# Top-k search of a sparse-attention block: two of six key blocks counted on ScalarE by the sign of the difference

## The chip, the cores and the metric

One core of one Trainium2 chip. The time is the device time of one execution, in microseconds (us); of several runs the median is given. Engines are named as in the profile: PE is TensorE's matmuls, PEld its weight loads, DVE is VectorE, ACT is ScalarE, POOL is GpSimd, SP is SyncE (it issues the loads).

## What is computed

Two layers of a conformer-like block with sparse attention, and after them a third block of another kind (a gated recurrence and an MLP), which the change does not touch. What matters here stands in the first two layers, for 1024 tokens:

```
conv:      y = silu(layernorm(causal_conv(u_val * sigmoid(u_gate)))) @ w_pw2 * silu(g_conv)
indexer:   score[t, s] = sum over 8 heads of w[t, h] * relu(q_idx[t, h] . k_idx[s]),  s <= t
           sel = top_k(score[t], 256)
attention: softmax over the 256 selected keys only
out:       [y_conv, y_attn] @ w_out, norm, gate, residual
```

Queries are worked on in 8 blocks of 128. In blocks 0 and 1 no query has more than 256 keys, so all are kept. For blocks 2 to 7 the 256th largest score of each query must be found among 384, 512, 640, 768, 896 and 1024 keys, and ties beyond it are cut by position.

## The kernel before

Each engine has a queue of its own, written out by hand, and semaphores between them. PE's order in a layer is: projections of the latents, the scores, then the convolution side (`conv_in` of wg and wv, two halves each of two tiles; `conv_turn(0)`, that is transposes xt 0 to 3; conv 0, 1; wv of the second half; conv 2, 3; `gates(0)`; `conv_turn(1)`, xt 4 to 7; conv 4, 5; `gates(1)`; conv 6, 7; `gates_by_token(0)`; conv 8, 9, 10; `gates_by_token(1)`; `normed_turn`; the four gemms of pw2; `out_half` of the convolution's output), and then the attention, which needs the selection.

Matrices are multiplied in three bf16 products of high and low halves. The weights come in chunks of 128x2048 in a ring of three, and POOL splits each chunk n into w_hi (4 casts, L506) and w_lo (4 subtractions, L510) once PE has used chunk n-3.

PSUM tiles are shared: `big` has two tiles of 1024 columns, taken in turn, and `c` has four banks. A tile can be taken again when its last reader is done. So wv half 0 tile 0 waits for ACT's sigmoid of wg half 0 tile 0 (`glu_gate(0, 0)`), the second half's wg tiles wait for DVE's `glu(0, 0)` and `glu(0, 1)`, the g tiles of `gates(0)` wait for `glu(1, 0)` and `glu(1, 1)`, xt 4 to 7 wait for `conv_out(0)` to `conv_out(3)`, conv 4 and 5 wait for `conv_x(4)` and `conv_x(5)`, and conv 8 to 10 wait for `conv_out(4)` to `conv_out(6)`.

The selection runs on DVE. `f` holds, for each query (128 partitions) and each of the 6 blocks (columns), the bits of the threshold found so far. For each of 31 bits, from the top, four things happen, each closed by `step()` (DVE waits for its own last write): the candidate, f with the bit flipped (L1642); `count`, which compares every score with the candidate and sums the hits, one instruction for each block, six in all (L1525); whether 256 were reached (L1644); the bit taken into f (L1645). Then comes one more count and, block by block, the pass that marks the selected keys (L1655 to L1659: five instructions over the block's full width).

Between the bits DVE does the convolution's work: `beside(slot)` is called before bit 30-slot, and `beside(32 + j)` before the pass of block j. `conv_x(4)` to `conv_x(7)` stand in slot 18, `conv_stats` in slot 26, `split_normed` (the low halves of the normed activations, on which pw2 waits) in slot 30, and `gated_convolution(0..3)` (on the last of which `out_half` waits) in slots 32 to 35, in front of the passes of blocks 2 to 5. ACT has no part in the search: it waits for PE's tiles, in the order glu_gate, conv_x, gate, gate_by_token, `L1129` (layer norm), silu, copies.

Of the kernel before, what the change touches and what calls it, by code (L numbers as in the profile page):

```python
# [23 lines left out]
P = 128  # L24
# [69 lines left out]
def build(nc, ap, events):  # L94

    ctx = ExitStack()
    with ctx:
# [49 lines left out]
        s_sq = ctx.enter_context(nc.semaphore("sq"))  # L147
        s_rb_out = ctx.enter_context(nc.semaphore("rb_out"))
# [168 lines left out]
        TBS = range(2, NT)  # L317
        sc_at = [0, 0]
# [670 lines left out]
        def _(act):  # L989
# [28 lines left out]
            for l in range(LAYERS):  # L1018
# [91 lines left out]
                for half in range(2):  # L1110
                    glu_gate(half, 0)
                    glu_gate(half, 1)
                for q in range(4):
                    conv_x(q)
# [239 lines left out]
        def _(dve):  # L1354
# [99 lines left out]
            for l in range(LAYERS):  # L1454
# [67 lines left out]
                def count(thr, op=ALU.is_ge):  # L1522
                    for j, tb in enumerate(TBS):
                        N = (tb + 1) * P
                        ins = dve.tensor_scalar(is_over[tb], score[tb], thr(j), 0.0, op, ALU.add, accum_out=cnt[:, j:j + 1])  # L1525
                    step(ins)
# [64 lines left out]
                def beside(slot):  # L1591
# [4 lines left out]
                    if slot == 5:  # L1596
                        glu(0, 0)
                    if slot == 7:
                        glu(0, 1)
                    if slot == 10:  # L1600
                        if l == 0:
                            ada(1)
                        conv_pad()
                        for q in range(4):
                            conv_x(q)
                    if slot == 11:
                        conv_out(0)
                        conv_out(1)
                    if slot == 12:
                        glu(1, 0)  # L1610
                    if slot == 14:
                        glu(1, 1)
                        conv_out(2)
                    if slot == 15:
                        conv_out(3)
                    if slot == 18:
                        for q in range(4, 8):
                            conv_x(q)
                    if slot == 19:
                        conv_out(4)  # L1620
                        conv_out(5)
                    if slot == 22:
                        conv_out(6)
                        conv_out(7)
                    if slot == 26:
                        conv_out(8)
                        conv_out(9)
                        conv_out(10)
                        conv_stats()
                    if slot == 27:  # L1630
                        conv_shift()
                    if slot == 30:
                        split_normed(0)
                        split_normed(1)
                        split_normed(2)
                        split_normed(3)
                    if 32 <= slot < 36:
                        gated_convolution(slot - 32)

                for bit in range(30, -1, -1):  # L1640
                    beside(30 - bit)
                    step(dve.tensor_scalar(cand, f, 1 << bit, None, ALU.bitwise_xor))  # L1642
                    count(lambda j: cand[:, j:j + 1].bitcast(F32))
                    step(dve.tensor_scalar(hit, cnt, TOPK - 0.5, float(1 << bit), ALU.is_ge, ALU.mult))  # L1644
                    step(dve.tensor_tensor(f, f, hit, ALU.bitwise_xor))  # L1645

                beside(31)
                count(lambda j: f[:, j:j + 1].bitcast(F32), ALU.is_gt)
                step(dve.tensor_scalar(s_(S_KEEP, nb), cnt, -1.0, TOPK + 0.5, ALU.mult, ALU.add))
                for j, tb in enumerate(TBS):  # L1650
# [8 lines left out]
                    step(dve.tensor_scalar(score[tb], eq, -1.0, NEG, ALU.add, ALU.mult))  # L1659

# [359 lines left out]
```

## Time and profile before

| | |
|---|---|
| median of 3 runs | 3466.71 us (3465.79 to 3471.36) |
| the profiled execution's own time | 3461.7 us |
| its span, first to last instruction | 3459.9 us |
| mean granted TensorE clock | 0.940 |
| PE busy | 3064.8 us (89% of the span) |
| DVE busy | 1953.9 us (56%) |
| POOL busy | 961.7 us (28%) |
| ACT busy | 893.7 us (26%) |
| of DVE: the search's counts, L1525, x384 | 337.9 us |
| search and passes, layer 0 | 248.8 to 587.3 us |
| search and passes, layer 1 | 1054.2 to 1357.2 us |

An engine's busy time is summed over all stages. What a stage costs is read from the wait that ends last in it, and in the stages with the search PE, DVE and POOL each wait for one another.

### The profile page before, as it was taken

Reading aid. Unit: us, or ns where it says so; the run is one execution under the profiler, and the core shown is the slowest. Engines: PE = TensorE matmul, PEld = TensorE weight load, DVE = VectorE, ACT = ScalarE, POOL = GpSimd, SP = SyncE. Lnnn points to the kernel's source line nnn. Section 1 sums busy time; section 2 is a strip of 40 time slices with the busy share of each in tenths; the row PEclk is TensorE's granted clock in tenths of the full one; section 3 lists DMA queues with packets and bytes.
Section 4 is the critical chain, followed back from the end, with each engine's and each line's share of the span. In section 5 each row is a group of like instructions: output and inputs, shape, how many; then the busy total and the mean of one; then the engine's idle time right before and its main releaser. Section 6 shows DMA issues by size and latency. Waiting matters only on the chain.

```text
span 3459.9 us, 48765 instructions
## 1 busy us (share of the span) xinstructions
PE 3064.8 (89%) x20177; PEld 1945.1 (56%) x20394; DVE 1953.9 (56%) x2977; ACT 893.7 (26%) x1544; POOL 961.7 (28%) x1046
## 2 busy tenths in 40 slices
PE   7889886988678977888699999999998899999997
PEld 7449762775338663875365465555555744444443
DVE  2586897564689996664636445365363433333334
ACT  2250022653351031653322222231221211010001
POOL 2201661002222661002232322322322223333330
PEclk9997998999799988999789999989999899999998
DMA  7222230001200330001211111111102111111101
GB/s 250 104 85 83 98 129 30 29 8 65 93 33 28 107 122 25 29 11 77 82 37 37 49 37 37 49 37 37 49 25 86 50 37 49 49 49 61 49 25 55
DMA packets 49165, 207.16 MB, mean 60 GB/s; under 512 B 4488, under 2 KB 9776, under 8 KB 32304
## 3 DMA queue, kind: packets, MB, share of 16 engines
q1 hardware_dynamic: 42288, 195.63, 16.0%
q10 hardware_dynamic: 6656, 8.39, 0.8%
q8 instruction: 162, 2.65, 0.3%
q14 instruction: 59, 0.48, 0.0%
HBM read 187.22 MB, written 16.79 MB: 59 GB/s over the span
## 4 chain that ended last, share of the span: by engine, by line
PE 68%; DVE 24%; issue 4%; ACT 2%; DMA 1%; POOL 1%; SPq 0%; DVEq 0%; ACTq 0%; POOLq 0%
PE big L264 15%; PE big L265 15%; PE big L263 15%; DVE arena L1525 6%; PE banks L263 4%; PE banks L264 4%; PE banks L265 4%; PE banks L948 3%; PE banks L821 2%; DVE arena L1683 2%; DVE arena L1515 2%; DVE arena L1410 1%; DVE arena L1691 1%; PE big L540 1%; PE banks L540 1%
## 5 line engine op out<-in xcount | busy, mean ns | idle before, releaser
L506 POOL CAST w_hi<-stage 128x512 bf16<-128x512 f32 x520 | 314.5, 647 | 2419.1 <-PE big L265 1742.9
L510 POOL TENSOR_TENSOR w_lo<-stage,w_hi 128x512 bf16<-128x512 f32 x520 | 652.5, 1285 | 0.0
L264 PE MATMUL big<-ht_lo,w_hi 128*128 128x512 bf16 x1381 | 527.5, 382 | 30.1 <-DVE ht_lo L1416 23.5
L265 PE MATMUL big<-ht_hi,w_lo 128*128 128x512 bf16 x1380 | 526.6, 382 | 1.4
L263 PE MATMUL big<-ht_hi,w_hi 128*128 128x512 bf16 x1359 | 518.4, 381 | 1.5
L263 PE MATMUL big<-w_hi,ht_hi 128*128 128x256 bf16 (+1 forms) x1274 | 386.1, 303 | 47.8 <-DVE ht_lo L1583 30.5
L264 PE MATMUL big<-w_lo,ht_hi 128*128 128x256 bf16 (+1 forms) x1274 | 385.9, 303 | 3.8 <-DVE ht_lo L1675 3.6
L265 PE MATMUL big<-w_hi,ht_lo 128*128 128x256 bf16 (+1 forms) x1276 | 386.1, 303 | 0.7 <-issue 0.4
L1525 DVE TENSOR_SCALAR_CACHE_REDUCE arena<-arena,smalli 128x384 bf16<-128x384 f32 (+5 forms) x384 | 337.9, 942 | 2.3
L263 PEld LDWEIGHTS big<-ht_hi,w_hi 128*128 128x128 bf16 x1408 | 140.4, 100 | 189.9 <-DVE ht_lo L1416 23.9
L265 PEld LDWEIGHTS big<-ht_hi,w_lo 128*128 128x128 bf16 x1408 | 138.7, 98 | 168.7 <-issue 4.7
L264 PEld LDWEIGHTS big<-ht_lo,w_hi 128*128 128x128 bf16 x1408 | 138.6, 98 | 162.6 <-issue 6.8
L263 PEld LDWEIGHTS big<-w_hi,ht_hi 128*128 128x128 bf16 x1280 | 151.8, 119 | 95.2 <-DVE ht_lo L1583 31.5
L263 PE MATMUL banks<-w_hi,arena 128*128 128x128 bf16 (+2 forms) x697 | 180.5, 278 | 22.8 <-DVE arena L1545 16.8
L264 PE MATMUL banks<-w_lo,arena 128*128 128x128 bf16 (+2 forms) x700 | 181.7, 279 | 0.4
L265 PE MATMUL banks<-w_hi,arena 128*128 128x128 bf16 (+2 forms) x699 | 181.2, 279 | 0.2
L263 PE MATMUL big<-w_hi,arena 128*128 128x256 bf16 (+1 forms) x509 | 166.9, 328 | 16.3 <-DVE arena L1870 16.1
L1228 ACT ACTIVATE arena<-big 128x1024 f32<-128x1024 f32 x64 | 65.5, 1023 | 446.7 <-PE big L265 446.5
L265 PEld LDWEIGHTS big<-w_hi,ht_lo 128*128 128x128 bf16 x1280 | 151.3, 118 | 41.4 <-issue 4.7
L264 PEld LDWEIGHTS big<-w_lo,ht_hi 128*128 128x128 bf16 x1280 | 151.2, 118 | 40.8 <-issue 3.9
L265 PE MATMUL big<-w_hi,arena 128*128 128x256 bf16 (+1 forms) x507 | 166.1, 328 | 0.3
L264 PE MATMUL big<-w_lo,arena 128*128 128x256 bf16 (+1 forms) x506 | 165.7, 328 | 0.2
(294 smaller groups left out, 5862.2 us busy)
## 6 DMA issues: line engine op xcount, KB each, us to landing
stage<-in_w SPq DMA_DIRECT2D x130, 1024.0 KB, 4.8
arena<-in_w_ada SPq DMA_DIRECT2D x48, 512.0 KB, 4.2
arena<-in_x SPq DMA_DIRECT2D x16, 512.0 KB, 7.1
xs<-arena SPq DMA_DIRECT2D x16, 512.0 KB, 2.6
arena<-xs SPq DMA_DIRECT2D x16, 512.0 KB, 7.9
gt<-arena ACTq DMA_DIRECT2D x16, 256.0 KB, 2.6
arena<-gt ACTq DMA_DIRECT2D x16, 256.0 KB, 2.7
out_x<-arena SPq DMA_DIRECT2D x8, 512.0 KB, 2.7
```

The lines of the kernel that those rows point to most:

```text
L263: pe.matmul(out, ah, bh, start=start, stop=False)
L264: pe.matmul(out, ah, bl, start=False, stop=False)
L265: return pe.matmul(out, al, bh, start=False, stop=stop)
L506: pool.tensor_copy(w_hi[:, n % RING, c0:c1], stage[:, n % RING, c0:c1]).then_inc(s_w_hi_split, mark(s_w_hi_split, n, q))
L510: ins = pool.tensor_tensor(w_lo[:, n % RING, c0:c1], stage[:, n % RING, c0:c1], w_hi[:, n % RING, c0:c1], ALU.subtract)
L540: ins = pe.matmul(g[:, (n * 4 + q) * 8 + k:(n * 4 + q) * 8 + k + 1], ada_buf(i)[:, k % 2, q * P:(q + 1) * P], s_(S_C + k), start=True, sto ...
L821: ins = pe.transpose(g[:, (s - q0) * P:(s - q0 + 1) * P], PB[h % 2][:, s * P:(s + 1) * P], ident)
L948: ins = pe.matmul(g[:, s * 64:(s + 1) * 64].rearrange("p (j h) -> p j h", h=h), KF[c][:, s * P:(s + 1) * P], q, start=True, stop=True)
L1228: act.activation(out, tile(pool, *key)[:, :], func, **kw).then_inc(s_read_act, mark(s_read_act, *key))
L1515: dve.scalar_tensor_tensor(score[tb], PB[i % 2][:, 0:N], w, score[tb], ALU.mult, ALU.add).then_inc(s_acc, mark(s_acc, l, i))
L1525: ins = dve.tensor_scalar(is_over[tb], score[tb], thr(j), 0.0, op, ALU.add, accum_out=cnt[:, j:j + 1])
L1683: dve.tensor_tensor_reduce(PB[h % 2][:, 0:N], tile("big", "lg", l, tb, h)[:, 0:N], mask_of(tb), 1.0, -NEG, ALU.add, ALU.min, s_(S_NMX + h ...
```

## The change

For blocks 6 and 7 (columns 4 and 5, 896 and 1024 keys) the count of each of the 31 bits moves to ACT: `Sign(candidate - score)` over the block's width with a summed output, two instructions for a bit. The sum is at most N - 2*256 + 1.5 when 256 scores or more lie above the candidate. DVE writes ACT's two candidates first and signals `s_cand`, counts its four blocks, and at the start of the next bit waits for `s_sign` and takes ACT's two counts into f (`sign_counts`: two comparisons of one column each, one xor). ACT passes through the 31 bits in its own queue, with the convolution's glu_gate and conv_x calls at fixed slots; gate(0), gate(1) and conv_x(4..7) come behind the last bit. Since a sum of signs counts an equal score by a half, an end on DVE follows for the two blocks: a count of all six blocks, `next_up` (12 small instructions), a count of the two, `at_least_f` (2), a count of the two again.

DVE's convolution work is placed anew: glu(0, 0) from slot 5 to 9, glu(0, 1) from 7 to 12, conv_x(0..3) from 10 to 18, conv_out(0) and (1) from 11 to 19 and 20, glu(1, 0) from 12 to 22, glu(1, 1) from 14 to 25, conv_out(2) and (3) from 14 and 15 to 27 and 28, conv_x(4..7) from 18 to 31, conv_out(4) and (5) from 19 to 33. conv_out(6) and all behind it (statistics, split_normed, gated_convolution) come after the last pass.

```
@@ ACT's queue: behind the relus of the scores @@
-                for half in range(2):
-                    glu_gate(half, 0)
-                    glu_gate(half, 1)
-                for q in range(4):
-                    conv_x(q)
+                def beside(slot):
+                    if slot == 4:
+                        glu_gate(0, 0)
+                    if slot == 7:
+                        glu_gate(0, 1)
+                    if slot == 15:
+                        glu_gate(1, 0)
+                    if slot == 17:
+                        glu_gate(1, 1)
+                    if slot == 18:
+                        for q in range(4):
+                            conv_x(q)
+
+                for bit in range(30, -1, -1):
+                    beside(30 - bit)
+                    act.wait_ge(s_cand, when(s_cand, l, bit))
+                    for j in ON_ACT:
+                        tb = TBS[j]
+                        ins = act.activation(is_over[tb], score[tb], ACT.Sign, scale=-1.0, bias=smalli[:, 8 + j:9 + j].bitcast(F32), accum_out=s_(S_CNT + j))
+                    ins.then_inc(s_sign, mark(s_sign, l, bit))
                 gate(0)
                 gate(1)
@@ DVE's queue @@
+                def next_up():
+                    up, lo, hi = [smalli[:, 24 + 8 * i:24 + 8 * i + a1 - a0] for i in range(3)]
+                    fa = f[:, a0:a1]
+                    step(dve.tensor_scalar(hit[:, a0:a1], cnt[:, a0:a1], TOPK - 0.5, None, ALU.is_ge))
...
+                    step(dve.tensor_tensor(fa, hi, lo, ALU.bitwise_or))
+
+                def at_least_f():
+                    keep = smalli[:, 24:24 + a1 - a0]
+                    step(dve.tensor_scalar(keep, cnt[:, a0:a1], TOPK - 0.5, -1.0, ALU.is_ge, ALU.mult))
+                    step(dve.tensor_tensor(f[:, a0:a1], f[:, a0:a1], keep, ALU.bitwise_and))
+
+                def sign_counts(bit):
+                    dve.wait_ge(s_sign, when(s_sign, l, bit))
+                    for j in ON_ACT:
+                        most = (TBS[j] + 1) * P - 2 * TOPK + 1.5
+                        ins = dve.tensor_scalar(hit[:, j:j + 1], cnt[:, j:j + 1], most, float(1 << bit), ALU.is_le, ALU.mult)
+                    step(ins)
+                    step(dve.tensor_tensor(f[:, a0:a1], f[:, a0:a1], hit[:, a0:a1], ALU.bitwise_xor))
 
                 for bit in range(30, -1, -1):
+                    if bit < 30:
+                        sign_counts(bit + 1)
+                    dve.tensor_scalar(cand[:, a0:a1], f[:, a0:a1], 1 << bit, None, ALU.bitwise_xor).then_inc(s_cand, mark(s_cand, l, bit))
                     beside(30 - bit)
-                    step(dve.tensor_scalar(cand, f, 1 << bit, None, ALU.bitwise_xor))
-                    count(lambda j: cand[:, j:j + 1].bitcast(F32))
-                    step(dve.tensor_scalar(hit, cnt, TOPK - 0.5, float(1 << bit), ALU.is_ge, ALU.mult))
-                    step(dve.tensor_tensor(f, f, hit, ALU.bitwise_xor))
+                    step(dve.tensor_scalar(cand[:, 0:a0], f[:, 0:a0], 1 << bit, None, ALU.bitwise_xor))
+                    count(lambda j: cand[:, j:j + 1].bitcast(F32), which=on_dve)
+                    step(dve.tensor_scalar(hit[:, 0:a0], cnt[:, 0:a0], TOPK - 0.5, float(1 << bit), ALU.is_ge, ALU.mult))
+                    step(dve.tensor_tensor(f[:, 0:a0], f[:, 0:a0], hit[:, 0:a0], ALU.bitwise_xor))
+                sign_counts(0)
 
                 beside(31)
-                count(lambda j: f[:, j:j + 1].bitcast(F32), ALU.is_gt)
+                thr_f = lambda j: f[:, j:j + 1].bitcast(F32)
+                count(thr_f, ALU.is_gt)
+                next_up()
+                count(thr_f, ALU.is_ge, ON_ACT)
+                at_least_f()
+                count(thr_f, ALU.is_gt, ON_ACT)
@@ behind the passes of the six blocks @@
+                conv_out(6)
+                conv_out(7)
+                conv_out(8)
+                conv_out(9)
+                conv_out(10)
+                conv_stats()
+                conv_shift()
+                for n in range(4):
+                    split_normed(n)
+                for n in range(4):
+                    gated_convolution(n)
```

## Rows read from the trace of the kernel before

**Rows 1.** Stages, by window: us; PE, PEld, DVE, ACT, POOL busy (instructions); PEclk; DMA share; GB/s

```profile
248.80:415.30 166.50, 158.36 (x1244) 142.44 (x1244) 126.07 (x289) 11.35 (x15) 60.58 (x72) 0.86 0.27 91
415.30:481.50 66.20, 61.38 (x586) 47.49 (x588) 59.95 (x131) 4.43 (x6) 42.22 (x52) 0.95 0.35 114
481.50:570.00 88.50, 50.98 (x318) 33.19 (x320) 82.42 (x135) 27.36 (x31) 34.17 (x37) 0.82 0.23 82
570.00:617.00 47.00, 46.43 (x236) 22.08 (x240) 16.79 (x15) 8.28 (x9) 9.46 (x13) 0.95 0.06 23
1054.20:1184.80 130.60, 115.73 (x1000) 102.72 (x1000) 125.97 (x284) 11.36 (x15) 59.68 (x72) 0.95 0.19 65
...
1252.80:1339.90 87.10, 51.22 (x319) 33.11 (x322) 81.22 (x135) 27.34 (x31) 33.38 (x36) 0.81 0.24 80
```

**Rows 2.** Waits, layer 0: engine, line <- releaser: us in total, times, longest

```profile
DVE arena L1666 <- ACT arena L1165: 30.8, 1, 30.8
...
PE big L263 <- DVE ht_lo L1583: 15.3, 1, 15.3
PE banks L263 <- DVE arena L1545: 6.8, 2, 6.0
PE big L263 <- POOL w_lo L510: 6.7, 2, 4.8
```

**Rows 3.** Timeline of DVE, one bit with POOL idle: start us, us

```profile
248.76 0.17 DVE L1642 TENSOR_SCALAR smalli<-smalli 128x6 int32<-128x6 int32 x1
248.97 0.61 DVE L1525 TENSOR_SCALAR_CACHE_REDUCE arena<-arena,smalli 128x384 bf16<-128x384 f32 x1
...
251.91 1.14 DVE L1525 TENSOR_SCALAR_CACHE_REDUCE arena<-arena,smalli 128x896 bf16<-128x896 f32 x1
...
254.29 0.17 DVE L1644 TENSOR_SCALAR smalli<-small 128x6 int32<-128x6 f32 x1
...
254.70 0.17 DVE L1642 TENSOR_SCALAR smalli<-smalli 128x6 int32<-128x6 int32 x1
```

**Rows 4.** Timelines of POOL and DVE, a bit under a weight split

```profile
430.16 4.50 POOL L510 TENSOR_TENSOR w_lo<-stage,w_hi 128x512 bf16<-128x512 f32 x4
...
431.15 0.20 DVE L1644 TENSOR_SCALAR smalli<-small 128x6 int32<-128x6 f32 x1
431.39 1.07 DVE L1645 TENSOR_TENSOR smalli<-smalli 128x6 int32<-128x6 int32 x1
432.49 1.08 DVE L1642 TENSOR_SCALAR smalli<-smalli 128x6 int32<-128x6 int32 x1
```

**Rows 5.** Timeline of DVE, layer 1: slot 18

```profile
1184.80 2.48 DVE L1545 TENSOR_TENSOR arena<-banks,arena 128x512 bf16<-128x512 f32 x4
```

**Rows 6.** Groups of ACT by shape: xcount | busy us, mean ns | idle before

```profile
L1206 ACT ACTIVATE arena<-arena,small 128x1024 f32<-128x1024 f32 x16 | 18.4, 1150 | 28.2 <-DVE small L1683 28.2
...
L1206 ACT ACTIVATE arena<-arena,small 128x896 f32<-128x896 f32 x16 | 16.7, 1043 | 23.3 <-DVE small L1683 23.3
```

**Rows 7.** Timelines of DVE and ACT, layer 0: PE's tiles arrive; a table load

```profile
296.55 1.23 DVE L1533 TENSOR_TENSOR arena<-big,arena 128x1024 f32<-128x1024 f32 x1 [13.80 <-PE big L265]
...
320.65 1.23 DVE L1533 TENSOR_TENSOR arena<-big,arena 128x1024 f32<-128x1024 f32 x1 [11.13 <-PE big L265]
...
351.91 1.02 ACT L1062 ACTIVATE arena<-big 128x1024 f32<-128x1024 f32 x1 [9.45 <-PE big L265]
...
354.91 1.28 ACT L1075 ACT_TABLE_LOAD   x1
```

**Rows 8.** Timeline of DVE, the selection pass of width 896

```profile
575.01 0.69 DVE L1655 TENSOR_SCALAR arena<-arena,smalli 128x896 f32<-128x896 f32 x1
...
580.17 0.63 DVE L1659 TENSOR_SCALAR arena<-arena 128x896 f32<-128x896 f32 x1
```

**Rows 9.** Timeline of POOL, a split beside the selection

```profile
557.32 6.89 POOL L510 TENSOR_TENSOR w_lo<-stage,w_hi 128x512 bf16<-128x512 f32 x4
```

**Rows 10.** Timeline of DVE, behind the batch statistics

```profile
487.38 12.22 DVE L1642 TENSOR_SCALAR smalli<-smalli 128x6 int32<-128x6 int32 x1
```

More of the change, by code:

```diff
@@ L317, in build @@
         TBS = range(2, NT)
+        ON_ACT = (NT - 4, NT - 3)
         sc_at = [0, 0]
@@ L1521, in _, with count @@
                 cnt = s_(S_CNT, nb)
-                def count(thr, op=ALU.is_ge):
-                    for j, tb in enumerate(TBS):
-                        N = (tb + 1) * P
+                on_dve = [j for j in range(nb) if j not in ON_ACT]
+                a0, a1 = ON_ACT[0], ON_ACT[-1] + 1
+                def count(thr, op=ALU.is_ge, which=range(nb)):
+                    for j in which:
+                        tb = TBS[j]
                         ins = dve.tensor_scalar(is_over[tb], score[tb], thr(j), 0.0, op, ALU.add, accum_out=cnt[:, j:j + 1])
@@ L1595, in beside @@
                         gate_gain(1)
-                    if slot == 5:
+                    if slot == 9:
                         glu(0, 0)
-                    if slot == 7:
+                    if slot == 12:
                         glu(0, 1)
-                    if slot == 10:
+                    if slot == 17:
                         if l == 0:
@@ L1612, in beside @@
                         glu(1, 1)
+                    if slot == 27:
                         conv_out(2)
-                    if slot == 15:
+                    if slot == 28:
                         conv_out(3)
-                    if slot == 18:
+                    if slot == 31:
                         for q in range(4, 8):
                             conv_x(q)
-                    if slot == 19:
+                    if slot == 33:
                         conv_out(4)
                         conv_out(5)
-                    if slot == 22:
-                        conv_out(6)
-                        conv_out(7)
@@ L1625, in beside @@
[L1625 to L1638, printed above, removed]
+                def next_up():
+                    up, lo, hi = [smalli[:, 24 + 8 * i:24 + 8 * i + a1 - a0] for i in range(3)]
+                    fa = f[:, a0:a1]
+                    step(dve.tensor_scalar(hit[:, a0:a1], cnt[:, a0:a1], TOPK - 0.5, None, ALU.is_ge))
+                    step(dve.tensor_scalar(up, fa, 31, None, ALU.arith_shift_right))
+                    step(dve.tensor_scalar(up, up, 2.0, 1.0, ALU.mult, ALU.add))
+                    step(dve.tensor_tensor(up, up, hit[:, a0:a1], ALU.mult))
+                    step(dve.tensor_scalar(lo, fa, 0xFFFF, None, ALU.bitwise_and))
+                    step(dve.tensor_tensor(lo, lo, up, ALU.add))
+                    step(dve.tensor_scalar(hi, fa, 16, None, ALU.arith_shift_right))
+                    step(dve.tensor_scalar(up, lo, 16, None, ALU.arith_shift_right))
+                    step(dve.tensor_tensor(hi, hi, up, ALU.add))
+                    step(dve.tensor_scalar(hi, hi, 16, None, ALU.logical_shift_left))
+                    step(dve.tensor_scalar(lo, lo, 0xFFFF, None, ALU.bitwise_and))
+                    step(dve.tensor_tensor(fa, hi, lo, ALU.bitwise_or))
```

10 lines of the change are left out of this document (7 added, 3 removed).

## The prediction

> **What bounds the kernel now.** I read the stage windows first, then PE's waits, then the timelines of DVE, POOL and ACT. The windows [rows 1] cut each layer at the same four places: the search's first bit, slot 18 (`conv_x(4)`), the end of conv 10, and the start of `out_half`. In layer 0 the stages take A 166.5, B 66.2, C 88.5 and D 47.0 us; in layer 1 A 130.6, B 68.0 (what lies between its neighbours) and C 87.1. DVE is busy 76% and 96% of A, 90% of B, 93% of C. Even so the selection is not what the attention waits for: in layer 0 the last pass ends at 587.3, and DVE's first instruction of the attention then idles 30.8 us [rows 2]. What counts is when DVE serves the convolution. PE waits 6.0 us for `conv_x(4)` (L1545, at the end of A), 15.3 us for the last `gated_convolution` (L1583, at the end of C) and up to 4.8 us for POOL's splits (L510) [rows 2]. So a faster search is worth nothing as such; the change is worth what its new order does to these three waits.
>
> **One bit.** With POOL idle a bit takes 254.70 - 248.76 = 5.94 us: the four narrow counts 251.91 - 248.97 = 2.94, the two wide ones 254.29 - 251.91 - 0.11 = 2.27, the last count's end 0.11, the three small steps 0.21, 0.21 and 0.20 [rows 3]. The change takes out 2.27 and adds four small instructions: two comparisons and the candidate for ACT, 0.1 each where nothing is waited for between them, and two closed steps of 0.2 that take one of these in; in sum 0.6. New bit: 5.94 - 2.27 + 0.6 = 4.27 us. ACT needs 1.04 + 1.15 for two activations of these widths with summed outputs and a pointer for bias, and 0.19 for the last read-out: 2.4 us [rows 6]. DVE works 3.7 us between sending ACT's candidates and wanting the sums, so ACT is hidden by 1.3 us, if Sign from SBUF costs what Exp from SBUF does. Without that cover each us beyond 3.7 would cost 62 us.
>
> **A bit under a split.** While POOL splits a chunk, each small instruction ends at the next end of a POOL instruction. POOL's subtractions come every 4.50 / 4 = 1.12 us, and the steps take 1.07 and 1.08 in place of 0.2; only the first, which falls in anywhere, took 0.20 [rows 4]. The counts are not held up. Casts come about every 0.56, so a POOL instruction is 0.84 on the mean. Now three small ones follow one another. Over A of layer 1, 130.6 us hold 18 bits (106.9), the work beside them (9.2) and a wait of some 2: 12.4 us are left for POOL's 59.7 us of work [rows 1]. That is 0.21 per us of POOL, or 1.55 per bit under a split, 0.52 for each small instruction. After the change seven follow one another: 7 x 0.52 = 3.6. A bit under a split costs 4.27 + 3.6 = 7.9, against 5.94 + 1.55 = 7.5 now. The bit that shrinks by 28% beside an idle POOL grows beside a busy one, and 46% of POOL's time (3.6 / 7.9) becomes delay. Only the one-column comparisons could escape, since no row has that shape; then five count, 2.6 a bit, 38%. I take seven, as the nearest row (six columns) waits.
>
> The Trainium skill, page "SBUF — State Buffer", section "Who interferes with whom", says that tensor_scalar, but not its accumulating form, and tensor_tensor with two SBUF inputs contend with GpSimd, and that the loser blocks for the whole instruction. The trace agrees with which ones wait (L1642 and L1645 1.08 and 1.07, L1525 0.61 as ever). By whole instructions, 7 x 0.84 less half of one for the first, less the 1.2 they take anyway, the delay is 4.2 a bit, and the forecast below would be some 4 us higher.
>
> **Stage A, layer 1.** `conv_x(4)` moves from slot 18 to slot 31. 31 x 4.27 = 132.4; beside it four glu (1.23 [rows 7] less an overlap of 0.1), conv_x 2.5 [rows 5], four conv_out at about 0.5: 9.1; POOL's work on the nine chunks up to g1, 60 us, at 46%: 27.6. Slot 31 comes at 1054.2 + 169.1 = 1223.3, against 1184.8 [rows 5]: +38.5. DVE waits for nothing in it; PE waits for glu(0, 0), glu(0, 1) and conv_x(0), which all come later than now. ACT then has a table load (1.28 [rows 7]), two Silu of the width of the sigmoid (1.02 [rows 7]) and a copy at 0.55 to do behind its last sum, of which 2 us stick out: **+40**.
>
> **Stage A, layer 0.** Here PE is slow to deliver. Slots 0 to 8: 9 x 4.27 + 2.3 (gate_gain) + 6.7 x 0.46 = 43.8, to 292.6; glu(0, 0) waits until 296.5 and glu(0, 1) until 320.6, for the same tiles as now [rows 7]. Slots 12 to 14 end near 337.6. In 15 and 17 ACT stands before wg tiles of the second half; the last comes at 351.9, then sigmoid 1.0 and the sums 2.4: slot 18 at 355.4. Thirteen bits 55.5, beside them 6.7, POOL's seven chunks less a part, 43.5 us, at 46%: 20. Slot 31 at 437.6, +2 as above, against 415.3: **+24**.
>
> **Stage B.** Between conv 4 and conv 10 PE is 93% busy [rows 1] and already waits for POOL. Now DVE's counts let POOL run. Afterwards this stage meets the end of the search: 12 + 2 small steps and, from about 20 us behind slot 31, the six passes, whose instructions are of the kind that contends, at full width. The pass of width 896 takes 5.8 us for five [rows 8]; by width all six take 27 us, 0.9 for each of the 30. Where such a pass meets a split now, POOL's four subtractions take 6.89 in place of 4.50 [rows 9], though the passes there are interrupted by instructions on PSUM. Uninterrupted, they alternate: a chunk of 8 instructions takes 6.7 + 8 x 0.9 = 14. The split of g2, for which PE waits, and those of cv8 and cv9, behind which cv10's queues, fall in here: **+7 and +7, +14 in each layer**, both for PE directly. The bound from below is 0, from the counts beside which POOL is not slowed; the passes are those of rows 9, so I take the whole.
>
> **Stage C.** Statistics, split_normed and gated_convolution no longer stand behind bits and passes. The low halves follow ACT's copies at once, the layer norm no longer waits for slot 27, and pw2 starts 5 us earlier; the 15.3 us before out_half shrink to the chain of one product (1.23), one copy (1.08) and one subtraction (1.15): 3.5. **-16** in layer 0, **-15** in layer 1. PE starts D behind a shorter idle time; 192 matmuls at 0.216 are 41.4 of the 47.0 us there, and I give back **-2** in each layer.
>
> **Sum.** Layer 0: 24 + 14 - 16 - 2 = +20. Layer 1: 40 + 14 - 15 - 2 = +37. The moves of glu and conv_out are in A; the semaphores cost nothing more (a satisfied wait shows no gap). No DMA is moved; the loads only follow POOL. +57 on the profiled execution's 3461.7 us gives 3519, and it ran 5.0 below the median of the runs, so 3524. With five small instructions A gives 3 and 5 less, 3516; own range 3508 to 3540.
>
> **Rivals.**
> - POOL is not held up by the passes: B costs 0, the sum is +29, 3496. For it: POOL's casts are hardly longer there. Against: rows 9. Chance 0.17.
> - The small steps don't queue (narrower shapes, or POOL's splits fall beside the counts): the other side. A gives +5 and +14, B 0, C and D as above: -16, 3451. It decides where a small step costs under 0.1 us for POOL, not 0.52, and the passes let POOL through. Against it: every burst in rows 4 waits. Chance 0.09.
> - Starvation: behind the batch statistics a small instruction waited 12.22 us until POOL ran out of work, past eight of its boundaries [rows 10]. ACT's candidate is followed directly by DVE's own. Should that pair starve the same way, a bit is held through each of POOL's runs: about another 60 us, 3580. Every other step behind an unclosed one waited for one boundary only. Chance 0.06.
> - ACT decides: a sum is late and DVE waits for it. If Sign and Sigmoid don't share a table, four slots a layer pay two loads of 1.28 and 1 for the sigmoid, of which 1.3 is covered: +2.3 x 8 = 18, 3542. The Trainium skill, page "ScalarE: Activation LUTs", section "Table sets: the hidden batching unit", says tables are switched by named sets at about 2.7 us; it doesn't list Sign. Chance 0.07.
>
> **How the numbers follow.** The forecast has 0.58, with 3524 its value; the remaining 0.03 is for no change by gains and losses that cancel. About 0.2% (7 us) is what a measurement here can tell. Slower is the sum of forecast, POOL let through, starvation and ACT: 0.88; faster 0.09; same 0.03. The range must leave out the other side and starvation; it reaches down to POOL let through and up to ACT: 3488 to 3546.
>
> **What the profile would show.** A new bit of 4.2 to 4.4 us beside an idle POOL, and 7 to 9 beside a busy one; two activations of 1.04 and 1.15; conv_x(4) at about 438 and 1224; PE's wait before conv 4 grown from 6 to some 20 us; a split of 12 us or more during the passes; PE's idle time before out_half down to 3.5. The prediction is wrong if bits under a split stay below 6 us, if ACT's sums are waited for, or if POOL's chunks keep 6.7 us.

## The result, and the profile after

The median goes from 3467.8 us (3465.8 to 3471.4, four runs) to 3490.5 us (3489.7 to 3495.8, four runs): a ratio of 1.0068, interval 1.0050 to 1.0085. The change costs 22.7 us. I had forecast 3524, so the direction was right and the size was not. The profiled execution of after took 3489.7 us (span 3487.9), 28.0 us of span more than before; the terms below are read from these two executions, and some 5 of the 28 are that before's ran 6 us under its median, after's only 1.

First the stages, cut where [rows 1] cut them: search's first bit, start of `conv_x(4)`, end of conv 10, start of `out_half`. Columns as there.

```profile
249.70:435.10 185.40, 161.63 (x1244) 145.39 (x1244) 154.71 (x485) 81.05 (x138) 60.67 (x72) 0.82 0.26 87
435.10:510.10 75.00, 63.19 (x586) 48.34 (x588) 64.97 (x75) 5.79 (x9) 59.66 (x53) 0.93 0.27 92
510.10:579.80 69.70, 50.25 (x318) 33.17 (x320) 24.43 (x31) 27.30 (x31) 28.56 (x34) 0.84 0.24 84
...
1059.40:1221.50 162.10, 116.82 (x1000) 102.19 (x1000) 153.55 (x479) 81.14 (x138) 60.81 (x72) 0.87 0.17 59
1221.50:1297.20 75.70, 64.17 (x586) 48.84 (x588) 66.28 (x76) 5.83 (x9) 60.97 (x53) 0.91 0.27 93
1297.20:1365.30 68.10, 48.59 (x318) 32.47 (x320) 25.18 (x31) 27.30 (x31) 28.13 (x34) 0.90 0.24 83
```

| stage | forecast, layers 0 and 1 | measured | 
|---|---|---|
| A, to conv_x(4) | +24, +40 | +18.9, +31.5 |
| B, to the end of conv 10 | +14, +14 | +8.8, +7.7 |
| C, to out_half | -16, -15 | -18.8, -19.0 |
| D, to the attention's first product | -2, -2 | -0.9, -0.2 |
| sum | +57 | +28 |

The sum of the measured terms equals the difference of the spans; what lies outside the four stages (+0.9 us ahead of layer 0, -3.7 between the layers, +2.8 behind) cancels. In B POOL is busy 59.7 us for the 42.2 of [rows 1], with the same chunks: the splits take longer there, which is already visible in one column.

Waits of layer 0 (engine, line, releaser: us in total, times, longest), to set beside [rows 2]:

```profile
PE banks L265 <- DVE arena L1565: 19.6, 2, 14.7
PE big L265 <- POOL w_lo L513: 9.8, 2, 5.7
...
PE banks L265 <- POOL w_lo L513: 5.1, 2, 4.0
PE big L265 <- DVE ht_lo L1603: 4.7, 1, 4.7
```

L1565 is `conv_x`: TensorE's wait before conv 4 grew from 6.0 to 14.7 us (in layer 1 from 4.9 to 15.2), and the one before conv 0 from 0.8 to 4.9 (in layer 1 from 5.1 to 14.4). L1603 is the last gated convolution: 15.3 became 4.7.

One bit beside an idle POOL (timeline of VectorE, start and duration), which took 5.94 in [rows 3]:

```profile
1059.37 0.17 DVE L1678 TENSOR_SCALAR smalli<-smalli 128x2 int32<-128x2 int32 x1
...
1062.91 0.16 DVE L1683 TENSOR_TENSOR smalli<-smalli 128x4 int32<-128x4 int32 x1
1063.10 0.21 DVE L1671 TENSOR_SCALAR smalli<-small 128x1 int32<-128x1 f32 x2
1063.35 0.16 DVE L1673 TENSOR_TENSOR smalli<-smalli 128x2 int32<-128x2 int32 x1
1063.55 0.17 DVE L1678 TENSOR_SCALAR smalli<-smalli 128x2 int32<-128x2 int32 x1
```

1063.55 - 1059.37 = 4.18 us. Now the same steps under a split, VectorE and then POOL, to set beside [rows 4]:

```profile
1181.53 0.53 DVE L1678 TENSOR_SCALAR smalli<-smalli 128x2 int32<-128x2 int32 x1
1181.97 0.65 DVE L1680 TENSOR_SCALAR smalli<-smalli 128x4 int32<-128x4 int32 x1
...
1185.70 0.27 DVE L1682 TENSOR_SCALAR smalli<-small 128x4 int32<-128x4 f32 x1
1186.01 1.07 DVE L1683 TENSOR_TENSOR smalli<-smalli 128x4 int32<-128x4 int32 x1
1187.11 0.21 DVE L1671 TENSOR_SCALAR smalli<-small 128x1 int32<-128x1 f32 x2
1187.36 0.83 DVE L1673 TENSOR_TENSOR smalli<-smalli 128x2 int32<-128x2 int32 x1
1188.22 0.53 DVE L1678 TENSOR_SCALAR smalli<-smalli 128x2 int32<-128x2 int32 x1
```

```profile
1181.42 2.29 POOL L509 CAST w_hi<-stage 128x512 bf16<-128x512 f32 x4
1183.67 4.50 POOL L513 TENSOR_TENSOR w_lo<-stage,w_hi 128x512 bf16<-128x512 f32 x4
```

This bit takes 1188.22 - 1181.53 = 6.69 us, not 7.9. Five steps are stretched, but the pair of one-column comparisons (L1671) is not: 0.21 to 0.22 us for both, in each of the 62 times that the two layers run it. No small step of a bit takes over 1.45 us in this trace. ScalarE's counts, beside it:

```profile
1182.09 1.04 ACT L1131 ACTIVATE arena<-arena,smalli 128x896 bf16<-128x896 f32 x1 [3.87 <-DVE smalli L1678]
...
1183.13 1.13 ACT L1131 ACTIVATE arena<-arena,smalli 128x1024 bf16<-128x1024 f32 x1
```

With the last read-out they end 1.3 us before VectorE's last count. Last, the splits beside the passes in layer 0, POOL and then VectorE:

```profile
463.88 3.54 POOL L509 CAST w_hi<-stage 128x512 bf16<-128x512 f32 x4 [9.80 <-PE big L267]
467.38 7.07 POOL L513 TENSOR_TENSOR w_lo<-stage,w_hi 128x512 bf16<-128x512 f32 x4
474.40 5.05 POOL L509 CAST w_hi<-stage 128x512 bf16<-128x512 f32 x4
479.42 7.61 POOL L513 TENSOR_TENSOR w_lo<-stage,w_hi 128x512 bf16<-128x512 f32 x4
486.98 4.86 POOL L509 CAST w_hi<-stage 128x512 bf16<-128x512 f32 x4
491.80 8.87 POOL L513 TENSOR_TENSOR w_lo<-stage,w_hi 128x512 bf16<-128x512 f32 x4
```

```profile
466.98 0.78 DVE L1699 TENSOR_SCALAR arena<-arena,smalli 128x640 f32<-128x640 f32 x1
467.80 2.33 DVE L1700 TENSOR_TENSOR_SCAN arena<-arena 128x640 f32<-128x640 f32 x1
470.16 1.59 DVE L1701 SCALAR_TENSOR_TENSOR arena<-arena,small 128x640 f32<-128x640 f32 x1
```

Three chunks take 10.6, 12.6 and 13.7 us instead of 6.7. The first is g2's, for which TensorE waits 5.7; the second is split while TensorE works on g2's four tiles (22.6 us) and costs nothing; of the third 1.1 sticks out, and for conv 10's chunk, queued behind it, TensorE waits 4.0. In before it waits 1.9 for g2's chunk and 1.9 for conv 10's. The net is 3.8 and, with the 1.1, 3.2 us; the remaining 1.8 of B's 8.8 is TensorE's own busy time, 63.2 for 61.4 us.

### The profile page after: what moved, and what is told of

It reads as the page before. It is cut to its first block, busy times and chain, and to the rows that moved or that the text cites. A ratio compares the mean times of both kernels' runs of the same rounds, so it can differ in the third digit from the quotient of the medians.

```text
span 3487.9 us, 49110 instructions
## 1 busy us (share of the span) xinstructions
PE 3070.3 (88%) x20177; PEld 1950.1 (56%) x20394; DVE 1873.4 (54%) x3021; ACT 1032.9 (30%) x1792; POOL 995.9 (29%) x1046
## 4 chain that ended last, share of the span: by engine, by line
PE 68%; DVE 21%; issue 5%; POOL 3%; ACT 2%; DMA 1%; SPq 0%; DVEq 0%; ACTq 0%; POOLq 0%
PE big L266 16%; PE big L267 15%; PE big L265 15%; DVE arena L1545 4%; PE banks L265 4%; PE banks L266 4%; PE banks L267 4%; PE banks L951 3%; PE banks L824 2%; POOL w_lo L513 2%; DVE arena L1738 2%; DVE arena L1533 2%; DVE arena L1428 1%; POOL w_hi L509 1%; DVE arena L1746 1%
## 5 line engine op out<-in xcount | busy, mean ns | idle before, releaser
L509 POOL CAST w_hi<-stage 128x512 bf16<-128x512 f32 x520 | 330.6, 679 | 2414.0 <-PE big L267 1702.2
L513 POOL TENSOR_TENSOR w_lo<-stage,w_hi 128x512 bf16<-128x512 f32 x520 | 671.0, 1322 | 0.0
L265 PE MATMUL banks<-w_hi,arena 128*128 128x128 bf16 (+2 forms) x697 | 182.0, 280 | 60.8 <-DVE arena L1565 49.3
L1545 DVE TENSOR_SCALAR_CACHE_REDUCE arena<-arena,smalli 128x512 bf16<-128x512 f32 (+5 forms) x268 | 206.7, 827 | 2.3
L1131 ACT ACTIVATE arena<-arena,smalli 128x896 bf16<-128x896 f32 x124 | 134.9, 1089 | 185.8 <-DVE smalli L1678 185.7
```

What stands on the lines that cost most here:

```text
L265: pe.matmul(out, ah, bh, start=start, stop=False)
L509: pool.tensor_copy(w_hi[:, n % RING, c0:c1], stage[:, n % RING, c0:c1]).then_inc(s_w_hi_split, mark(s_w_hi_split, n, q))
L513: ins = pool.tensor_tensor(w_lo[:, n % RING, c0:c1], stage[:, n % RING, c0:c1], w_hi[:, n % RING, c0:c1], ALU.subtract)
L1131: ins = act.activation(is_over[tb], score[tb], ACT.Sign, scale=-1.0, bias=smalli[:, 8 + j:9 + j].bitcast(F32), accum_out=s_(S_CNT + j))
```

## The experiments

Ratios are to the kernel before, from runs on the same chip; the kernel after stands at 1.0068. The runs were spread over several chips, so two of them are compared by their ratios (0.001 is 3.5 us) rather than by their medians.

| run | median us | ratio, interval |
|---|---|---|
| e1 passes last | 3477.0 | 1.0015 (1.0000 to 1.0029) |
| e2 before, passes last | 3442.2 | 0.9918 (0.9896 to 0.9939) |
| e3 two columns | 3497.2 | 1.0074 (1.0054 to 1.0094) |
| e4 one column | 3510.4 | 1.0112 (1.0090 to 1.0134) |
| e5 planned | 3424.8 | 0.9874 (0.9858 to 0.9889) |
| e6 planned, candidates by column | 3425.1 | 0.9871 (0.9850 to 0.9893) |
| e7 no exact end | 3483.6 | 1.0037 (1.0013 to 1.0060) |
| e8 planned, VectorE alone | 3433.9 | 0.9918 (0.9896 to 0.9939) |
| e9 before, statistics closed | 3465.4 | 0.9999 (0.9984 to 1.0015) |
| e10 e8 refitted | 3432.2 | 0.9911 (0.9896 to 0.9926) |
| e11 e5 refitted in layer 1 | 3425.3 | 0.9889 (0.9873 to 0.9906) |
| e12 e10 refitted | 3430.5 | 0.9890 (0.9874 to 0.9907) |

### Stages B and C: where the passes stand (e1, e2)

e1, on the kernel after:

```
                 count(thr_f, ALU.is_gt, ON_ACT)
                 step(dve.tensor_scalar(s_(S_KEEP, nb), cnt, ...))
-                for j, tb in enumerate(TBS):    # the six passes
-                    ...
+                conv_out(4)
+                conv_out(5)
                 conv_out(6)
                 ...
                 for n in range(4):
                     gated_convolution(n)
+                for j, tb in enumerate(TBS):
+                    ...
```

> Edit on the kernel after: the six selection passes move behind the four gated convolutions; the low convolution outputs 4 and 5 come behind the exact end. Theory (the passes hold up POOL's splits between conv 4 and conv 10): that stretch, 74.1 us in layer 0 and 74.8 in layer 1 in the kernel after against 65.3 and 67.1 in the kernel before, falls back to about 66 and 67; the passes (27 us) fit beside out_half, where VectorE idles 47 us; the total falls by about 16 us, to some 3474. Rival (the stretch is longer for another reason, the exact end's small steps or TensorE's clock): the stretch stays at 74 and the total within 5 us of the kernel after.

Measured 3477.0, by the ratios 18 us below after, where some 16 were expected. Stages A and B of layer 0, by window, and the four subtractions of a split in B, from POOL's timeline:

```profile
248.20:429.00 180.80, 157.27 (x1246) 141.00 (x1244) 156.01 (x485) 81.14 (x138) 60.68 (x72) 0.84 0.27 90
429.00:496.80 67.80, 63.17 (x588) 48.33 (x588) 26.04 (x45) 5.76 (x9) 42.75 (x53) 0.93 0.29 99
```

```profile
466.82 4.50 POOL L513 TENSOR_TENSOR w_lo<-stage,w_hi 128x512 bf16<-128x512 f32 x4
```

B falls from 75.0 to 67.8 (68.2 in layer 1), POOL's time in it from 59.7 to 42.8, a chunk is back at 6.7, while C (70.3 and 68.4) keeps its gain. In layer 0 1.6 us over before's 66.2 are left, and before's own B took 67.7 us in the trace of e2, whose B is unchanged: B's cost was the passes, as far as this can tell. A is the same code as after and took 180.8 here against 185.4: in this execution TensorE's second wv tile held VectorE for 7.1 us, in after's for 10.3. Layer 0's term A is therefore known to some 5 us only; layer 1's is 162.0 and 162.1.

e2, on the kernel before:

```
-                    if 32 <= slot < 36:
-                        gated_convolution(slot - 32)
...
+                for n in range(4):
+                    gated_convolution(n)
                 for j, tb in enumerate(TBS):    # the six passes
```

> Edit on the kernel before: the passes of all six blocks move behind the four gated convolutions, nothing else. Theory (what the change gains in stage C is that nothing stands between gated convolutions, and ScalarE's counting has no part in it): TensorE's wait before out_half falls from 15.3 to about 4.7 us in each layer, and the total by some 21 us, to about 3446. Rival (the wait is set by the search's 31 bits, which still end at 535, so that the chain through the layer norm is late): less than 5 us per layer.

Measured 3442.2, 27 us below before on the same chip, where 21 were expected. From TensorE's waits in layer 0:

```profile
PE big L263 <- DVE ht_lo L1583: 4.7, 1, 4.7
```

The 15.3 us are 4.7 without any count on ScalarE. From the end of conv 10 to out_half e2 takes 76.9 us in layer 0, 11.6 less than before, and 11.6 less in layer 1; the change gained 18.8 and 19.0. So 11.6 us of the gain in C came from the order of VectorE's queue, and before could have had them alone. The other 7, most of them from pw2 starting earlier, e2 does not give.

### Stage A: which small steps POOL holds up (e3, e4)

e3 and e4, on the kernel after:

```
# e3
-    ins = dve.tensor_scalar(hit[:, j:j + 1], cnt[:, j:j + 1], most, float(1 << bit), ALU.is_le, ALU.mult)
+    ins = dve.tensor_scalar(smalli[:, 48 + 2 * i:50 + 2 * i], cnt[:, a0:a1], most, float(1 << bit), ALU.is_le, ALU.mult)
# e4, and so for every small step of a bit
-    step(dve.tensor_tensor(f[:, 0:a0], f[:, 0:a0], hit[:, 0:a0], ALU.bitwise_xor))
+    for j in on_dve:
+        ins = dve.tensor_tensor(f[:, j:j + 1], f[:, j:j + 1], hit[:, j:j + 1], ALU.bitwise_xor)
+    step(ins)
```

> Edit on the kernel after: each of the two comparisons of ScalarE's sums runs over two columns instead of one, into a scratch tile. Theory (an instruction of one column escapes the queue with POOL, one of two columns does not): beside an idle POOL nothing changes (4.18 us a bit); beside a busy one the pair, now 0.21 us for both, takes 1 to 2 us; a bit under a split goes from 6.5 to about 7.6, the start of conv_x(4) moves by 4 us in layer 0 and 6 in layer 1, and the total rises by about 10 us. Rival (the pair escapes by its place or its data types, float in and integer out): the pair stays at 0.21 us and the total unchanged.

> Edit on the kernel after: every small step of a bit (candidates, comparisons, xors) is written as one instruction per column. Theory (one column escapes): a bit costs 4.18 plus about 1.1 for 11 more instructions, 5.3 us, beside an idle and a busy POOL alike, against 4.18 and 6.5 now; POOL's splits are not stretched; conv_x(4) comes some 10 us later in layer 1 and the total rises by 10 to 20 us. Rival (the comparisons escaped by place or type): single columns of the xors wait too, several boundaries of 1.1 us in each bit, 10 us and more for a bit under a split, and the total rises by over 40 us.

e3 took 3497.2. e4 took 3510.4, 20 us above after by the medians and 15 by the ratios, within its 10 to 20, with 4.8 us a bit beside an idle POOL where I had said 5.3. The pair in e3, under a split and then beside an idle POOL:

```profile
1191.05 1.08 DVE L1671 TENSOR_SCALAR smalli<-small 128x2 int32<-128x2 f32 x2
...
1198.98 0.24 DVE L1671 TENSOR_SCALAR smalli<-small 128x2 int32<-128x2 f32 x2
```

A bit's steps in e4, under a split:

```profile
1197.21 0.34 DVE L1689 TENSOR_SCALAR smalli<-small 128x1 int32<-128x1 f32 x4
1197.58 3.77 DVE L1692 TENSOR_TENSOR smalli<-smalli 128x1 int32<-128x1 int32 x4
...
1202.62 0.33 DVE L1685 TENSOR_SCALAR smalli<-smalli 128x1 int32<-128x1 int32 x4
```

Width decides for `tensor_scalar`: in one column it never waits (no group of four over 0.34 us), in two columns the same comparison takes up to 2.2 us for the pair. Layer 1's stage A is 1226.1 - 1060.0 = 166.1 us in e3 against 162.1: 4 of the 8.5 us by which I overstated it. (The total of e3, 1.0074, cannot be told from after's 1.0068; the stage can.) But one column does not free a `tensor_tensor`: four xors took 3.77 us, each but the first waiting for one more end of a subtraction of POOL (every 1.12 us). Both rival lines of e4 were half right. The Trainium skill has this in two places, "VectorE: DVE Perf Modes", section "What auto-detection actually checks" (the mode that uses both ports asks that source and destination have outermost non-unit dimensions that are even, or equal; one column, as I read it, has none) and "SBUF — State Buffer", section "Who interferes with whom" (`tensor_scalar` contends in those modes only, `tensor_tensor` with both inputs in SBUF without them). The traces agree with both; the prediction weighed the second page and left out its condition on `tensor_scalar`.

e6 uses it, on e5 below:

```
-    dve.tensor_scalar(cand[:, a0:a1], f[:, a0:a1], 1 << bit, None, ALU.bitwise_xor).then_inc(s_cand, ...)
+    for j in ON_ACT:
+        ins = dve.tensor_scalar(cand[:, j:j + 1], f[:, j:j + 1], 1 << bit, None, ALU.bitwise_xor)
+    ins.then_inc(s_cand, ...)
```

> Edit on e5_planned: the candidates (a tensor_scalar of two columns and one of four) are written as six of one column. Theory (a tensor_scalar of one column is not held by POOL, as the comparisons of 0.21 us for two show): beside an idle POOL a bit costs 0.2 us more, beside a busy one some 1.2 less; over 31 bits, nine of them under splits, 4 us less in a layer where the bits set the end, so 0 to 8 us less in all. Rival (the comparisons escape for another reason than their width): 0.2 x 31 = 6 us more per layer, up to 12 in all.

The candidates indeed never waited (0.21 to 0.22 us for two, up to 0.33 for four, in all 62 bits), and a bit beside an idle POOL became 4.4 us. The total cannot be told from that of e5. What the form is worth stays open: the five executions lie between 3411.8 and 3432.2 us, and in the profiled one, the slowest, two comparisons behind the counts took 8.76 and 7.58 us (see the section on the order, and the last).

### The exact end (e7)

The lines from `next_up()` to the last `count(thr_f, ALU.is_gt, ON_ACT)` are left out.

> Edit on the kernel after: the exact end (the 12 small steps, the two further counts of two blocks, the two steps of at_least_f) is left out, so that a threshold of blocks 6 and 7 can be off by one step where scores are equal; the first count of all six blocks stays. Theory (its 15 us lie on VectorE behind conv_x(4..7), where TensorE waits for nothing from it; it only shifts the passes against POOL's splits): the total within 5 us of the kernel after, and the passes hold up the split of g2 by more, those of cv8 and cv9 by less. Rival (it is on the path): 10 to 15 us less in each layer, 3465.

Measured 3483.6, 6.9 below after by the medians and 11 by the ratios, more than the 5 expected, though the two intervals still overlap. The passes start earlier and meet g2's split with their wide blocks: TensorE waits 8.2 us for it instead of 5.7, and 1.9 for conv 10's chunk instead of 4.0, as expected. From `conv_x(4)` to out_half the two layers take 144.6 and 143.5 us, in after 144.8 and 143.8. So in these stages the exact end costs 0.3 us at most; if the total did fall by more, this trace does not show where.

### The order fitted to TensorE, with and without ScalarE's counts (e5, e8, e10, e11, e12)

e5, on e1. The two tables name, for each layer, what is done beside which slot:

```
+PLAN_DVE = ({15: glu 0 0, 17: glu 0 1, 22: pad, x 0-3, 23: out 0, 26: out 1, glu 1 0, glu 1 1, out 2,
+             28: out 3, 30: x 4-7, out 4, out 5},
+            {7: glu 0 0, glu 0 1, pad, 12: x 0-3, 14: out 0, out 1, 17: glu 1 0, glu 1 1, out 2,
+             22: out 3, 24: x 4-7, 30: out 4, out 5})
+PLAN_ACT = ({3: gate 0 0, 11: gate 0 1, 21: gate 1 0, 22: gate 1 1, x 0-3, 30: g 0, g 1, x 4-7},
+            {0: gate 0 0, 3: gate 0 1, 10: gate 1 0, 12: gate 1 1, x 0-3, 22: g 0, g 1, 23: x 4-7})
+# behind the bits: out 6-10, conv_stats, conv_shift, the exact end, split_normed, gated_convolution, passes
```

> Edit on the kernel after: ScalarE still counts two blocks and the passes come last, as in the run e1_passes_last; the convolution's work is placed anew, in each layer by itself, so that glu, conv_x and conv_out come when TensorE's tiles are ready: conv_x(4..7) behind 30 bits in layer 0 and behind 24 in layer 1, glu(0, 1) in slot 17 and 7; ScalarE's gates and conv_x calls move with them; the exact end goes behind the layer norm's shift, where VectorE idles 20 us for ScalarE. Theory (what the change lost, it lost by the slots at which VectorE serves TensorE): TensorE's wait before conv 4, 14.7 and 15.2 us, falls to under 6 in layer 0 and under 10 in layer 1, conv 4 starts near 412 in layer 0, out_half starts some 35 and 25 us earlier than in the kernel after; total 3415, within 10. Rival (ScalarE's waits for TensorE's tiles inside the bits hold its sums, and VectorE with them): bits of over 8 us around those slots and a total over 3440.

Measured 3424.8, at the edge of the expected 10 around 3415: 46 us below before on the same chip, some 66 below after; this version beats both kernels. Stages A to C of layer 0, and TensorE's waits in layer 1:

```profile
249.50:412.40 162.90, 160.21 (x1247) 143.06 (x1244) 146.31 (x471) 78.98 (x134) 55.31 (x67) 0.85 0.28 93
412.40:476.00 63.60, 59.08 (x590) 44.96 (x588) 11.59 (x25) 7.98 (x13) 47.42 (x58) 1.00 0.36 120
476.00:545.70 69.70, 49.33 (x320) 32.61 (x320) 38.45 (x67) 27.32 (x31) 29.31 (x35) 0.90 0.25 88
```

```profile
PE banks L265 <- DVE arena L1562: 12.8, 2, 9.1
...
PE big L265 <- ACT arena L1080: 5.2, 1, 5.2
```

In layer 0 TensorE waits under 1 us for `conv_x(4)`, and in B the granted clock is 1.00, which is 2.4 GHz throughout, where it was 0.93 behind the wait of 14.7 us. Out_half starts 296 us behind the first bit instead of 330. In layer 1 9.1 us are left before conv 4.

e8 does the same with before's six counts on VectorE, e10 and e12 refit it where TensorE was seen to wait; e11 refits e5 in layer 1.

> Edit on the kernel before: VectorE counts all six blocks as ever and ScalarE has no part in the search; only VectorE's convolution work is placed anew, in each layer by itself (conv_x(0..3) from slot 10 to 14 and 9, conv_x(4..7) from 18 to 19 and 16, outputs 8 to 10 and the statistics at 27 and 24, the low halves at 30 and 29), and the passes come behind the gated convolutions. Theory (the order alone brings the gain of e5_planned, and the counts on ScalarE bring nothing): 3420, within 10, no slower than e5_planned (3425). Rival (31 bits of 5.94 us leave no order that serves both the middle and the layer norm in time): no better than e2_before_passes_last (3442).

> Edit on e8_planned_dve, in which TensorE waited 16.2 us for output 6 in layer 0 and 17.1 and 6.5 us for the low halves in layer 1: outputs 4, 5 come at slot 22 and 6, 7 at 25 in layer 0, output 5 at 19 and the low halves at 27 in layer 1, glu(0, 0) at 11 in layer 0. VectorE still counts all six blocks. Theory (the order is worth the whole gain): those waits shrink to about 5, 9 and 0, total 3412, within 10, below e5_planned. Rival (six counts on VectorE leave it too full: each slot moved makes another one late): 3430 or more.

> Edit on e10_planned_dve2 (VectorE counts all six blocks), where TensorE waited 17.2 us in layer 1 for a gated convolution that stood behind the last bits: there gated_convolution(0) and (1) come at slots 29 and 30, and the last count of all blocks comes behind the gated convolutions in both layers. Theory (the counts on ScalarE are worth nothing once the order is fitted): the 17.2 us fall to 2 or less, out_half of layer 1 starts some 15 us earlier, total 3417 within 8, ratio about 0.987 as for e5_planned and e11_planned2. Rival (VectorE with six counts stays the bound there, and gives the wait back elsewhere): 3428 or more, a ratio of 0.990 or more.

> Edit on e5_planned (two blocks counted on ScalarE), layer 1 alone: conv_x(0..3) at slot 11 instead of 12, outputs 0 and 1 at 13, glu(1, 0), glu(1, 1) and output 2 at 16, output 3 at 21, conv_x(4..7) at 22 instead of 24, and ScalarE's gate(2) and gate(3) in front of its slots 27 and 29 instead of behind all bits. Theory: TensorE's waits of 3.8 (conv 0), 9.1 (conv 4) and 5.2 us (gates_by_token) fall to about 1, 4 and 0; total 3412, within 8. Rival (ScalarE's waits inside the bits hold its sums and VectorE): 3425 or more. Against e10_planned_dve2 it tells what the counts on ScalarE are worth when both orders are fitted: this theory says nothing, within 10 us.

Their edits are entries of those tables only, but for e12, in which two gated convolutions go among the last bits and the last count goes behind them:

```
-                for n in range(4):
+                for n in ((0, 1, 2, 3), (2, 3))[l]:
                     gated_convolution(n)
+                count(lambda j: f[:, j:j + 1].bitcast(F32), ALU.is_gt)
+                step(dve.tensor_scalar(s_(S_KEEP, nb), cnt, -1.0, TOPK + 0.5, ALU.mult, ALU.add))
```

e8, e10 and e12 took 3433.9, 3432.2 and 3430.5: the theory's 3412 to 3420 was missed each time, and e11's 3412 too, with 3425.3. Layer 1 of e12, TensorE's waits:

```profile
PE banks L263 <- DVE arena L1555: 9.6, 1, 9.6
...
PE big L263 <- DVE ht_lo L1584: 9.3, 1, 9.3
...
PE big L263 <- DVE arena L1581: 4.1, 1, 4.1
```

The 17.2 us of e10 (L1581, gated convolution) became 4.1, and 9.6 for output 6 and 4.6 more before out_half came in their place. e11 went the same way: 9.1, 3.8 and 5.2 us became 4.3, 0.8 and 4.1, and new waits of 5.2 (a glu) and 3.9 (an output) appeared. With ScalarE's counts the two fitted orders stand at 0.9874 and 0.9889, without them the best two at 0.9890 and 0.9911. The best intervals overlap, so these runs put the worth of ScalarE's counts between nothing and some 13 us, against over 30 for the order.

The waits that I fitted the orders to were in large part not waits for the order. A step can starve, as in [rows 10]: it is not served until POOL has run out of work. The comparison behind the counts did so in e8, e12 and e6, one line from each (timeline of VectorE):

```profile
476.41 7.45 DVE L1622 TENSOR_SCALAR smalli<-small 128x6 int32<-128x6 f32 x1
```

```profile
1196.63 9.13 DVE L1624 TENSOR_SCALAR smalli<-small 128x6 int32<-128x6 f32 x1
```

```profile
424.02 8.76 DVE L1667 TENSOR_SCALAR smalli<-small 128x4 int32<-128x4 f32 x1
```

In e8 this step stands right before output 6, for which TensorE waited 16.2 us, and another of 8.04 us before it; a step of 11.4 us behind the statistics of layer 1 stands before the low halves (17.1). In e10 such a step of 12.2 us stands before the wait of 17.2. In layer 1 of e12 VectorE is busy without a gap from the 9.13 us to output 6, for which TensorE waited 9.6. In e5 no small step of a bit takes over 1.22 us, but in e11, also with ScalarE's counts, two take 5.9. With one trace of each, these runs cannot separate what a fuller queue costs from what such steps cost, so the 13 us are no measure of the counts alone.

### The starved step of rows 10 (e9)

```
                 ins.then_inc(s_stats, mark(s_stats, "var", l))
+                dve.wait_ge(s_stats, when(s_stats, "var", l))
```

> Edit on the kernel before: VectorE waits for its own last bn_aggr before it goes on, nothing else. Theory (the small step of rows 10 starves for 12.2 us because it is issued behind an instruction that is not closed, while POOL works): that step takes 1.1 us or less; slots 27 to 31 and the gated convolutions come 10 us earlier, TensorE's wait before out_half falls from 15.3 to about 5 in each layer, total 3447. Rival (it starves by its place beside the splits, whatever closes the work before it): 12 us again, in the wait or behind it, and the total unchanged.

```profile
495.63 0.64 DVE L1564 BATCH_NORM_AGGREGATE diag<-diag 128x2 f32<-128x6 f32 x8
496.30 12.11 DVE L1643 TENSOR_SCALAR smalli<-smalli 128x6 int32<-128x6 int32 x1
```

Measured 3465.4 and a step of 12.11 us (11.28 in layer 1): my theory fell. See the last section.

## Why the prediction was right in sign and twice too large

**The bit.** Forecast 4.27 beside an idle POOL, measured 4.18; over 31 bits that is 2.8 us a layer.

**The failed step: "I take seven, as the nearest row (six columns) waits", and with it 7.9 us for a bit under a split.** In stage A of layer 1, 162.1 us are 31 x 4.18 = 129.6, the work beside the bits 9.1 and 2.2 of waiting for ScalarE's copy; 21.2 are left for POOL's 60.8: 0.35 us of delay for each us of POOL, not 0.46, and a bit under a steady split is 4.18 / 0.65 = 6.4. The forecast had 27.6 for these 21.2. The direct test is e3: widening the pair to two columns gives 4 of the missing 8.5 us back. The price of five, which stood in the prediction as its lower case (21 and 35), was the nearer one. In layer 0 the term was 24 for 18.9.

**Stage B** had the right mechanism (e1 removes it, to within 1.6 us) at 14 us a layer instead of 8.8 and 7.7. I charged g2's split and conv 10's with a full alternation (14 us a chunk). g2's met the narrow passes, at 10.6; of the delay of the two chunks before conv 10's most was hidden by TensorE's 22.6 us on g2's tiles, which I had not set against it. Net of before's waits the two cost 3.8 and 3.2 us in layer 0, where I had 7 and 7.

**Stage C** went as forecast and 3 to 4 us further: pw2 starts 5.9 us nearer to the end of the gates by token, out_half's wait falls by 10.6, and within pw2 a wait of 1.3 us for a gated convolution is gone as well, with TensorE's slow stretch behind it: 22.2 instead of 24.2 us.

**ScalarE** was hidden, as forecast (1.04 and 1.13 us). Among the bits it loads a table once in a layer, 1.28 us at the first sigmoid; Sign behind it needs none, so the rival of two loads at four slots fell. Each load seen took 1.28 us, as in [rows 7], not the about 2.7 that the prediction quotes. In layer 0 its sums are late once, by 8.4 us, because the sigmoid ahead waits for TensorE's tile, as worked out for slot 17. The prediction had both this wait in its sum and "if ACT's sums are waited for" among the signs of being wrong; the second was worded too widely. The band of 7 to 9 us for a bit under a split was missed (6.69), and the wait before conv 4 was put at some 20 us for 14.7 and 15.2. Of the rivals, POOL let through by the passes (3496) came nearest in time, and for a wrong reason: e1 shows that the passes do hold POOL up. Starvation did not come in after's bits (no step over 1.45 us), though it did in other versions. Of the step in [rows 10] the prediction says that it passed eight of POOL's boundaries; by POOL's timeline, counting casts and subtractions, they are thirteen.

**The two errors in A and B have one sign** because both priced contention by its worst row. Together they make 25 of the 29 us between the forecast sum and the measured one; C gives 7 more, D takes 3 back.

## What to carry to other kernels

Price a hand-written queue by the deadlines of the engine that bounds the kernel: moving work off VectorE was worth at most some 13 us here, serving TensorE's tiles when they came and putting the passes where nothing waited for them was worth over 30, in the old kernel as in the new. When a step can be cheap or dear by its shape and no row has that shape, look up which condition makes it so before taking the nearest row. Where two engines exclude each other, ask for each delayed transfer what it hides behind: of three stretched splits one was free. And before an order is changed because of a wait, look for a single stretched instruction ahead of it: e10 and e12 answered waits that had one.

## What the runs showed of the hardware

- A `tensor_scalar` of one column is never held by POOL (0.21 us for two, 0.34 at most for four), one of two columns is; a `tensor_tensor` of one column is held as well (3.77 us for four).
- Starvation (rows 10) is not due to the unclosed instruction ahead (e9, 12.11 us). In e5 a step behind the reciprocal, right before a count, starved too, for 3.40 us:

```profile
490.47 0.20 DVE L1586 RECIPROCAL diag<-diag 128x8 f32<-128x8 f32 x1 [8.50 <-ACT diag L1140]
490.71 3.40 DVE L1588 SCALAR_TENSOR_TENSOR diag<-diag 128x8 f32<-128x8 f32 x1
```

```profile
489.59 4.48 POOL L515 TENSOR_TENSOR w_lo<-stage,w_hi 128x512 bf16<-128x512 f32 x4
```

It ended at 494.1, as POOL's run of splits did, past two ends of its subtractions. Nor is it tied to what stands ahead: behind `bn_aggr` it came in before and in each version on it (in at least one layer), behind the reciprocal in after and in each version on it (2.4 to 3.7 us), and behind the read-out of a count in e2, e6 and e8 to e12 (up to 14.15 us in e12). In the two layers of all these traces, every single step of up to 16 columns that took over 2 us ended with POOL's run of splits. In most bits the same comparison at the same place waits for one instruction of POOL or for none. What makes a step miss every chance stays open.
- TensorE's clock in stage B went with its wait before conv 4: behind under 1 us it was granted 0.97 to 1.00 (layer 0 of e5, e10, e11 and e12), behind 6.0 and 4.9 us 0.95 and 0.94 (before), behind 14.7 and 15.2 us 0.93 and 0.91 (after). Stage B holds other waits too, so this is no measure of the one wait alone.
